# Attention: the second head's maximum beside the first head's exponential; the shared key's tile in two passes of 64 columns

## What is computed

```
proj = u @ w_in            # c_q, c_kv, k_pe (32 columns, shared by all heads), HGRN2 columns, gates
k_pe = apply_rope(k_pe, cos, sin)
s = einsum('bqhd,bkhd->bhqk', qn, k_nope) + einsum('bqhd,bkd->bhqk', qp, k_pe)
s = where(k_idx <= q_idx, s * scale, -inf)
p = softmax(s)                      # over the keys
o = einsum('bhqk,bkhd->bqhd', p, v)
```

## Time and profile before

| what | value |
|---|---|
| median of 3 runs | 1494.26 us |
| lowest and highest | 1493.94 and 1495.15 us |
| the profiled execution, its own time | 1496.1 us |
| its span, first to last instruction | 1494.4 us |
| TensorE busy (weight loads) | 1377.6 us (983.6) |
| VectorE, ScalarE, GpSimd busy | 581.8, 561.4, 101.6 us |
| mean granted clock | 0.98 |

### The profile page before, as it was taken

One profiled execution on the slowest core, in us unless ns is written; L12 is line 12 of the kernel. 1 busy time (PEld: TensorE's weight loads), 2 busy tenths in 40 slices (PEclk: granted clock), 3 DMA queues, 4 the chain that ended last, 5 costly groups with the idle time before them and its releaser, 6 DMA issues. The chain is left out here.

```text
span 1494.4 us, 21048 instructions
## 1 busy us (share of the span) xinstructions
PE 1377.6 (92%) x8471; PEld 983.6 (66%) x8471; DVE 581.8 (39%) x1303; ACT 561.4 (38%) x1066; POOL 101.6 (7%) x131
## 2 busy tenths in 40 slices
PE   5999999999999999999999999999987878688786
PEld 5888887787888887666667888855544444344442
DVE  6455565432531054656677556411110111111117
ACT  6534355222322146444552355533322222222223
POOL 0000000000000000000000011311111111111100
PEclk9999999999999999989999999999999999999998
DMA  6111111112234333112137654999999999999998
GB/s 185 43 29 43 29 29 43 30 32 78 80 97 122 101 89 124 57 36 71 36 120 240 253 194 157 321 416 415 415 416 416 416 417 416 416 416 417 415 403 333
DMA packets 130433, 312.53 MB, mean 209 GB/s; under 512 B 31120, under 2 KB 77200, under 8 KB 113184
## 3 DMA queue, kind: packets, MB, share of 16 engines
q1 hardware_dynamic: 118304, 285.96, 51.2%
q0 software_dynamic: 12032, 25.22, 4.4%
HBM read 283.81 MB, written 41.98 MB: 218 GB/s over the span
## 5 line engine op out<-in xcount | busy, mean ns | idle before, releaser
L2397 PE MATMUL ps<-r,m_xT 128*64 128x256 f32 x2048 | 253.4, 403 | 68.2 <-DMA r<-in_w 67.6
L130 PE MATMUL ps<-uTh,h_wh 128*128 128x512 f32 (+3 forms) x696 | 263.8, 379 | 4.4 <-DVE uTl L566 2.4
L131 PE MATMUL ps<-uTl,h_wh 128*128 128x512 f32 (+3 forms) x696 | 255.9, 368 | 0.0
L132 PE MATMUL ps<-uTh,h_wl 128*128 128x512 f32 (+3 forms) x696 | 255.6, 367 | 0.0
L2397 PEld LDWEIGHTS ps<-r,m_xT 128*64 128x64 f32 x2048 | 150.6, 145 | 153.5 <-DMA r<-in_w 76.1
L130 PEld LDWEIGHTS ps<-uTh,h_wh 128*128 128x128 f32 (+1 forms) x696 | 129.4, 186 | 28.7 <-DVE uTl L566 4.3
L2313 DVE TENSOR_TENSOR m_prod<-m_sig,ps 128x128 f32<-128x128 f32 x64 | 18.4, 288 | 333.4 <-ACT m_sig L2284 333.4
L132 PEld LDWEIGHTS ps<-uTh,h_wl 128*128 128x128 f32 (+1 forms) x696 | 129.3, 186 | 20.1
L131 PEld LDWEIGHTS ps<-uTl,h_wh 128*128 128x128 f32 (+1 forms) x696 | 129.6, 186 | 19.5 <-issue 0.2
L2379 PE MATMUL ps<-r,m_hT 128*64 128x512 f32 x512 | 122.4, 598 | 1.3 <-DVE m_hT L2317 0.9
L2274 ACT ACTIVATE m_y<-ps,gate 64x512 f32<-64x512 f32 x128 | 87.4, 682 | 80.0 <-PE ps L2379 78.4
(11 more groups left out here) (363 smaller groups left out, 2098.7 us busy)
## 6 DMA issues: line engine op xcount, KB each, us to landing
r<-in_w SPq DMA_DIRECT2D x190, 1024.0 KB, 24.3
h_w<-in_w_in SPq DMA_DIRECT2D x37, 512.0 KB, 4.3
gates<-h_sg POOLq DMA_DIRECT2D x16, 512.0 KB, 2.9
r<-y_moe SPq DMA_DIRECT2D x8, 1024.0 KB, 17.1
br_gate<-gates SPq DMA_DIRECT2D x14, 512.0 KB, 4.1
e_wo<-in_w_out SPq DMA_DIRECT2D x4, 1024.0 KB, 6.1
f_x<-in_x SPq DMA_DIRECT2D x8, 512.0 KB, 5.1
h_mid<-f_x SPq DMA_DIRECT2D x8, 512.0 KB, 4.5
```

Of the source, the lines that this page charges most:

```text
L130: pe.matmul(out, lh, rh, start=start, stop=False)
L131: pe.matmul(out, lh, rl, start=False, stop=False)
L132: return pe.matmul(out, ll, rh, start=False, stop=stop)
L2397: ins = pe.matmul(bank(UP_BANK + e % 2, 0, DE, CAP * f, CAP * (f + 1)).rearrange("p (r f) -> p r f", r=2), xT[i % 2][:, j, CAP * k:CAP * ( ...
```

## The change

Two edits. In the attention VectorE's queue holds, in every step, the mask and maximum of head 1 ahead of the reciprocal and scaling of head 0. In the job `p` the low part of the weights is written beside the high part, in columns 32 to 63 of the same tile, and each piece is made by two products per row group instead of three, with 64 stationary columns: one moves the high part of the stream and one the low part. Rows 0 to 31 of the bank then hold high x (high + low), rows 32 to 63 low x (high + low). ScalarE copies the first 32 rows as before and raises `pp_ok`; VectorE adds the other 32 rows to them (`summed_p`) and raises `p_ok`, which frees the bank.

```diff
@@ scalar, piece
-                    act.activation(kpe[0:ROPE, c:c + m], bank(p % 3, 0, m, ROPE), ACT.Copy).then_inc(p_ok, 1)
+                    act.activation(kpe[0:ROPE, c:c + m], bank(p % 3, 0, m, ROPE), ACT.Copy).then_inc(pp_ok, 1)
@@ vector, low
-                dve.tensor_tensor(used(wl, J), used(w, J), used(wh, J).bitcast(F32), ALU.subtract).then_inc(wl_ok, 1)
+                low_part = wh[J % 2][:, :, ROPE:2 * ROPE] if JOBS[J][0] == "p" else used(wl, J)
+                dve.tensor_tensor(low_part, used(w, J), used(wh, J).bitcast(F32), ALU.subtract).then_inc(wl_ok, 1)
@@ vector
+            def summed_p(n):
+
+                c0, m = cols_of(LAT + 5)[n]
+                at_bank = spot[LAT + 5, n] % 3 * 512
+                dve.wait_ge(pp_ok, n + 1)
+                dve.tensor_tensor(kpe[0:ROPE, c0:c0 + m], kpe[0:ROPE, c0:c0 + m],
+                                  g.ps[ROPE:2 * ROPE, at_bank:at_bank + m], ALU.add).then_inc(p_ok, 1)
...
+                    if B == HG and s in (27, 29):
+                        summed_p(s // 2 - 13)
+            summed_p(2)
@@ tensor, half
+                if JOBS[J][0] == "p":
+
+                    for j in range(4 * y, 4 * y + 4):
+                        for u_one in (g.uTh, g.uTl):
+                            last = pe.matmul(bank(p % 3, 0, m, 2 * ROPE), wh[J % 2][:, j, 0:2 * ROPE], u_one[:, j, col:col + m],
+                                             start=j == 0 and u_one is g.uTh, stop=j == DK - 1 and u_one is g.uTl)
@@ attention, vector
-                if k + 2 == len(steps):
+                if more:
 
                     peak(k + 1, 1)
                     normed(k + 1, 0)
-                    normed(k + 1, 1)
-                elif more:
-                    normed(k + 1, 0)
-                    peak(k + 1, 1)
                     normed(k + 1, 1)
```

More of the change, by code:

```diff
@@ L211, in project_part @@
         sg_out = [sem(f"h_sg_out{b}") for b in range(2)]
+        pp_ok = sem("h_pp_ok")
         raw_ok, p_ok, ns_ok, ms_mm, nr_ok, n_ok, nh_ok, nl_ok = (
@@ L840, in half @@
                 col, m = cols_of(J)[n]
-                rows = ROPE if JOBS[J][0] == "p" else P
                 if cols_of(J) is REAL:
                     col += META
-                for j in range(4 * y, 4 * y + 4):
-                    last = mm3(pe, bank(p % 3, 0, m, rows), wh[J % 2][:, j, 0:rows], wl[J % 2][:, j, 0:rows], g.uTh[:, j, col:col + m],
+                if JOBS[J][0] == "p":
[3 more added lines that the diff above has]
+                                             start=j == 0 and u_one is g.uTh, stop=j == DK - 1 and u_one is g.uTl)
+                for j in range(4 * y, 4 * y + 4) if JOBS[J][0] != "p" else ():
+                    last = mm3(pe, bank(p % 3, 0, m), wh[J % 2][:, j, :], wl[J % 2][:, j, :], g.uTh[:, j, col:col + m],
                                g.uTl[:, j, col:col + m], j == 0, j == DK - 1)
```

## The result

| | median | runs | lowest to highest |
|---|---|---|---|
| before | 1494.66 us | 4 | 1493.94 to 1495.15 |
| changed | 1479.42 us | 4 | 1478.55 to 1479.95 |

The ratio is 0.9898, with a 95% interval of 0.9881 to 0.9915: about 15 us less, where 13.0 were forecast (1481.3). The profiled execution after took 1479.6 us with a span of 1477.9. A second set of four runs of the same kernel gave a median of 1479.19.

What follows compares the result with a forecast made beforehand. The prediction took TensorE's own path ahead of the DMA-bound experts as the limit: 9.2 us from the attention plus 3.8 from the key's tile make 13.0, giving 1481.3 us against the median of 1494.26, range 1478 to 1486.

Steps and rivals of the forecast that it cites:

- The attention: Attention steps: head 1's maximum ahead of head 0's scaling removes TensorE's waits before transposes, 9.2 us less over four head pairs.
- the second pair repeats it, 2.9, with its first steps at half clock: Attention, second head pair: gains the same 2.9 us as the third pair, though its first steps run at half clock.
- the key's tile: Shared key's tile: 16 products of 64 columns instead of 24 of 32 in each of three pieces, 3.8 us less.
- rival C: Half-clock stretch behind the 144 small products: its length changes, moving the time 2.6 us either way; 12 in 100.
- The rule of the Trainium skill: Shared key's tile: weight loads overlap products only across row groups, making the saving 4.7 us; the forecast kept 3.8.
- A: Attention: head 0's chain becomes the bound and steps pay beyond 0.4 us of margin; 3 in 100, plus 2 near no change.
- the turning point at 0.9 of excess: Attention: the whole gain is gone if head 0's chain exceeds the forecast by 0.9 us in some 26 steps.
- margin of 0.4: Attention, steps i=1 to i=6: head 0's scaling can come 0.4 to 0.5 us later before TensorE waits.
- B: Attention: the wait moves to ScalarE's queue, leaving half the attention gain, 1485.9 us; 13 in 100.
- the 0.3 that was left for ScalarE's copies: Attention, step i=7: head 1's transposes still wait for ScalarE's two copies, leaving 0.3 us of the 1.35 lost.
- D: Shared key's tile gives nothing: 64 columns cost half as much again or the gate's first product waits, 1485.1 us; 3 in 100.
- the stages behind would pass the gain on: DMA-bound experts' part: weight loads issue in program order, so it starts earlier by the whole 13.0 us gain.

## Why the prediction was right

**The attention: 9.2 forecast, 9.3 outside the clock's stretch and 0.2 in it at an equal clock.** The weight loads that open steps k = 0, 7 and 10 in the kernel before (k = 31 is in the earlier trace rows), and then those of k = 0, 7, 10 and 31 in the changed one:

```profile
579.15 0.14 PEld L1328 LDWEIGHTS ps<-ident,t_p 112*128 112x128 f32 x1
...
620.17 0.86 PEld L1328 LDWEIGHTS ps<-ident,t_p 128*128 128x128 f32 x8 [0.17 <-issue]
...
649.20 0.31 PEld L1328 LDWEIGHTS ps<-ident,t_p 128*128 128x128 f32 x3 [0.17 <-issue]
```

```profile
575.75 0.14 PEld L1342 LDWEIGHTS ps<-ident,t_p 112*128 112x128 f32 x1
...
614.99 0.86 PEld L1342 LDWEIGHTS ps<-ident,t_p 128*128 128x128 f32 x8 [0.17 <-issue]
...
640.87 0.31 PEld L1342 LDWEIGHTS ps<-ident,t_p 128*128 128x128 f32 x3 [0.17 <-issue]
...
762.95 0.86 PEld L1342 LDWEIGHTS ps<-ident,t_p 128*128 128x128 f32 x8 [1.07 <-DVE t_p L1259]
```

From k = 0 to 7 and from k = 10 to 31 that is 41.02 + 129.64 = 170.66 us before and 39.24 + 122.08 = 161.32 after: 9.3 less. The second profiles give 170.62 and 161.37, the attention edit alone 161.33. For the same steps the forecast had 1.5 in the first pair, 1.19 + 1.05 in the second from i=2 on, 2.9 and 1.9, so 8.5, and they gave 0.8 more: 1.8 in the first pair (41.02 - 39.24; small waits that no row gives were left out), 129.64 - 122.08 - 3.0 - 1.9 = 2.7 in the second from i=2 on, 48.08 - 45.10 = 3.0 in the third, 40.61 - 38.68 = 1.9 in the last. The 2.7 is over 2.24 because of step k = 10 itself, whose second turn waited 1.14 us:

```profile
650.92 0.31 PEld L1328 LDWEIGHTS ps<-ident,t_p 128*128 128x128 f32 x3 [1.14 <-DVE t_p L1241]
```

Without the last queries' products the same turn waits 0.73, and the second pair gains 2.2 from i=2 on. So of what the old order loses behind the stretch, 0.4 us shows one step later, outside it.

**The step that was mis-sized: "the second pair repeats it, 2.9, with its first steps at half clock".** It put 0.76 - 0.1 = 0.66 us into the steps between k = 7 and k = 10. The profiles take 29.0 and 27.5 us there before (27.5 too with the key's tile or the unused semaphore alone), and 25.9 and 27.3 after (27.4 with the attention edit alone). So at an equal 3.4 us of withheld clock the order brings 0.2, 0.5 less than forecast, and without the stretch it brings 21.63 - 19.84 = 1.8. That the attention's total is off by only 0.3 is luck in part: 0.8 too little outside the stretch and 0.5 too much in it nearly cancel (the rows gave 9.5 in all against 9.2).

On top the stretch itself differs by run, which is rival C: 5.1 and 3.4 us withheld before, 1.7 and 3.45 after. The other runs add to this. With the old order the unused semaphore and the key's tile alone show 3.4 each. With the new order it is 3.4 in the attention edit alone and in the run with the mask added four times, and 1.7 in the run with the mask added twice and in that with the low part moved. The mean is 3.8 us in four profiles of the old order and 2.6 in six of the new (the half pieces one step later, with a gap ahead of these products, had 6.8). In one and the same kernel 1.7 us withheld cost 1.5 us (29.0 against 27.5 us), so the difference would be worth about 1.1 us, an estimate. That is the size of what the sum below leaves open, but ten profiles are too few to show that the new order meets a short stretch more often.

**A second stretch, at the start of the merging.** It has the same habit, and the forecast didn't have it. The kernel before withheld 0.34 x 5 = 1.7 us there in its first profile and nothing in its second:

```profile
785.00:790.00 5.00, 3.90 (x11) 3.12 (x12) 0.00 (x0) 0.00 (x0) 2.36 (x12) 0.66 0.56 172
```

```profile
785.00:790.00 5.00, 4.98 (x22) 4.13 (x23) 1.38 (x2) 0.00 (x0) 2.36 (x12) 1.00 0.79 252
```

The changed kernel does the same, 1.7 us in its first profile and nothing in its second. From the first turn of k = 31 to the experts' first gather it is 177.93 and 177.45 us before, 178.58 and 177.35 after. These 1.2 us between two executions of one kernel are no effect of the change, and they limit what two single profiles can show.

**The key's tile: right.** The last copy starts at 345.53 before and 342.00 after, 3.5 us earlier. The copy ahead of the tile starts at 334.18 and 334.43, so the execution after was 0.25 us late already, and the tile itself brings 3.8. Of this 0.1 is lost again on the way to the attention: from the last copy to its first turn it is 579.15 - 345.53 = 233.62 us before and 575.75 - 342.00 = 233.75 after. So 3.7 arrive. The 16 products of a piece in 2.55 us are 0.16 us each, as before.

The rule of the Trainium skill ("TensorE: Matmul & The Clock Gate", section "The mechanism") gave 4.7 as the prediction took it, that a load overlaps products in flight only when it goes to another row group; by that rule, the trace does not agree. The same section also lets a load go ahead of products in flight when it is for the background weight buffer; no run here shows which buffer these loads used.

**What the forecast didn't have.** VectorE's last instruction, in the kernel before and after:

```profile
1487.88 1.28 DVE L2344 SCALAR_TENSOR_TENSOR r<-r,z_stat,r 128x1024 f32<-128x1024 f32 x1
```

```profile
1472.32 1.28 DVE L2358 SCALAR_TENSOR_TENSOR r<-r,z_stat,r 128x1024 f32<-128x1024 f32 x1
```

From its end to the end of the span pass 1494.4 - 1489.16 = 5.2 us before and 1477.9 - 1473.60 = 4.3 after. The 5.2 is in all five profiles without the key's edit, the 4.3 in all eight with it. So the edit brings 0.9 us at the far end of the program, 1130 us later, and 3.7 + 0.9 = 4.6 is most of what was measured of it alone (4.9). The unused semaphore doesn't bring it. The traces show what goes with it. These are the DMA packets from that point to the end of the span, before and then after (the row of the queue that the profile calls instruction, which the kernel after doesn't have there: queue, packets, MB, share; and the last write of the output, with the us from issue to landing):

```profile
q14 instruction: 1, 0.01, 0.4%
...
out<-r SPq DMA_DIRECT2D x1, 512.0 KB, 3.6
```

```profile
out<-r SPq DMA_DIRECT2D x1, 512.0 KB, 2.6
```

Before, one packet of the instruction queue falls into the last write of the output (at 1491.0 to 1491.3 us), and that write lands 3.6 us after its issue. After, that queue's last packet comes at 1468.0 to 1468.6, ahead of the last write, which lands in 2.6. The packet and the 3.6 are in all five profiles without the key's edit, neither is in the eight with it. That the edit moves this packet by changing the number of instructions (21048 before, 21003 after) is likely and not shown.

**The rivals.** A (head 0's chain as the bound) didn't happen, and its price was right: 0.98 us more on the chain, and the change is worse than nothing, where the forecast put the turning point at 0.9 of excess. Its margin of 0.4 held but for i=2. B (the wait moves to ScalarE) didn't happen: i=7 kept 0.33 us, the 0.3 that was left for ScalarE's copies. C happened in part: the stretch was shorter after than before in the first profiles, and equal in the second. D didn't happen: the copies come 2.55 us apart and the first gate's product was not late (its copy starts 5.60 us behind the tile's last in both kernels). That the stages behind would pass the gain on was right: from the merging's last sum to the experts' first gather it is 123.9 us before and after. That gather starts at 956.77 before and 941.53 after, 15.2 us earlier, where the last step of the attention starts 15.9 earlier (in the second profiles 13.1 and 13.0); the 0.65 between went to the merging, which takes 46.0 to 47.5 us from profile to profile, in either order.

**The sum.** 9.3 for the steps outside the stretch, 0.2 in it, 3.7 for the tile and 0.9 at the end are 14.1 of the 15.2 us; 1.1 stay open. That the forecast of 13.0 came out 2.2 us short is so the end's 0.9, which no row of before pointed to, and this 1.1; its attention and tile were off by 0.2 together. A shorter stretch in the new order would fill the 1.1 (the estimate above), but it isn't the whole of it: without the last queries' products there is no stretch, and the same sum gives 8.9 + 1.8 + 3.7 + 0.9 = 15.3 us where 16.1 were measured. There 0.75 us of the difference of the two profiles lies between the first turn of k = 31 and the gather, where the clock differs by execution. What the 1.1 us are stays open.

## What to carry to other kernels

When two chains share an in-order queue, put what feeds the other engine next ahead of what it needs only a step later, and ask by how much the delayed one still comes in time: here a margin of 0.4 us in nearly all steps carried a gain of 9 us, and 1 us more on that chain would have turned it into a loss. Compare how long whole steps last, not the sum of gaps: the gaps said 25.6 us, the steps 10. Before moving anything else (the low part, the half pieces), find who needs it within the same step; both moves looked free and cost 7 and 12 us.

## What was not expected of the hardware

The changed program met 1.7 and 3.45 us of withheld clock in two executions, and the program before 5.1 and 3.4, behind the same 144 small products; at the start of the merging each had 1.7 us once and nothing once. The Trainium skill says in "TensorE: Matmul & The Clock Gate", section "Part 1: The HAM clock gate", that the point at which the clock comes back varies from run to run, as it isn't tied to the program: by that rule, the traces agree. And the span's last stretch, behind the last instruction of any engine that computes, took 5.2 or 4.3 us, nothing in between: an edit in the first third of the program decided whether one packet of the instruction queue, of 0.01 MB, fell into the last write of the output.
